# Sixteen of 22 blocks of each down projection as four jobs of seven products, with weight sums formed in DRAM

## The reference, cut to what matters

```python
def swiglu(hn, w_gate, w_up, w_down):
    return (jax.nn.silu(hn @ w_gate) * (hn @ w_up)) @ w_down   # w_down: 2816 x 1024
```

## Time and profile before

| | us |
|---|---|
| median of 3 runs | 2952.11 (2951.89 to 2953.47) |
| the profiled execution | 2952.24 |
| its span, first to last instruction | 2950.4 |
| TensorE busy in it | 2920.0 (99%) |
| VectorE, ScalarE, GpSimd busy | 1885.0, 1424.0, 1150.5 |
| DMA | 289.05 MB, mean 98 GB/s |

### The profile page before, as it was taken

The page is one execution under the profiler, slowest core; times in us unless marked ns, Lnnn a source line. Parts: engine busy times, 40 slices in busy tenths (PEclk is TensorE's granted clock), DMA queues, the critical chain, the costliest instruction groups (busy, mean ns, idle before and its releaser), DMA issues.

```text
span 2950.4 us, 44030 instructions
## 1 busy us (share of the span) xinstructions
PE 2920.0 (99%) x16942; PEld 2469.7 (84%) x16942; DVE 1885.0 (64%) x2718; ACT 1424.0 (48%) x2327; POOL 1150.5 (39%) x798
## 2 busy tenths in 40 slices
PE   8999999999999999999999999999999999999998
PEld 7778887799997877788888898988787888889987
DVE  7974333497885978772116888668777520288883
ACT  6443344455534546664234556344566532355553
POOL 5336575410124533234455214254332354541242
PEclk9999999999999999999999999999999999999999
DMA  5344343233323523223323234254231233333322
GB/s 163 86 115 138 94 129 103 75 115 104 97 81 87 148 72 102 55 72 89 97 90 105 78 113 127 79 123 135 70 94 48 71 97 98 97 97 100 101 94 79
DMA packets 221965, 289.05 MB, mean 98 GB/s; under 512 B 43466, under 2 KB 135682, under 8 KB 219970
## 3 DMA queue, kind: packets, MB, share of 16 engines
q1 hardware_dynamic: 219266, 281.07, 32.5%
q0 software_dynamic: 880, 2.99, 0.3%
q10 hardware_dynamic: 1616, 2.23, 0.2%
HBM read 270.98 MB, written 4.72 MB: 93 GB/s over the span
## 4 chain that ended last, share of the span: by engine, by line
PE 92%; DVE 5%; ACT 2%; issue 1%; POOL 0%; DMA 0%; SPq 0%; ACTq 0%; DVEq 0%
PE half L1063 66%; PE half L1392 4%; PE half L1394 4%; PE half L1395 4%; PE half L1581 2%; PE half L1595 2%; PE half L1559 1%; PE half L1466 1%; PE half L1468 1%; PE half L1469 1%; PE half L1564 1%; PE half L1657 0%; DVE arena L2752 0%; PE half L1318 0%; PE half L1335 0%
## 5 line engine op out<-in xcount | busy, mean ns | idle before, releaser
L4014 POOL TENSOR_TENSOR wL<-slot,wH 128x512 fp32r<-128x512 f32 x776 | 1125.0, 1459 | 1771.2 <-ACT wH L1781 1769.8
L1781 ACT ACTIVATE wH<-slot 128x512 fp32r<-128x512 f32 x776 | 475.4, 622 | 814.0 <-PE half L1063 786.4
L1063 PE MATMUL half<-nH,wH 128*128 128x512 f32 x1728 | 684.7, 396 | 4.2 <-ACT arena L1794 2.3
L1063 PE MATMUL half<-nH,wL 128*128 128x512 f32 x1728 | 673.5, 390 | 0.0
L1063 PE MATMUL half<-nL,wH 128*128 128x512 f32 x1728 | 673.3, 390 | 0.0
L1063 PE MATMUL half<-arena_split,wH 128*128 128x512 f32 (+1 forms) x2048 | 617.6, 384 | 0.8 <-POOL wL L4014 0.3
L1063 PEld LDWEIGHTS half<-arena_split,wH 128*128 128x128 f32 x2048 | 378.9, 188 | 78.6 <-POOL wL L4014 2.6
L1063 PEld LDWEIGHTS half<-nH,wH 128*128 128x128 f32 x1728 | 324.4, 188 | 87.1 <-issue 18.5
L1063 PE MATMUL half<-arena_split,wL 128*128 128x512 f32 (+1 forms) x1024 | 391.7, 383 | 0.0
L1063 PEld LDWEIGHTS half<-nH,wL 128*128 128x128 f32 x1728 | 324.4, 188 | 69.2
L1063 PEld LDWEIGHTS half<-nL,wH 128*128 128x128 f32 x1728 | 324.7, 188 | 65.4 <-issue 1.4
(11 more groups left out here) (480 smaller groups left out, 5287.7 us busy)
## 6 DMA issues: line engine op xcount, KB each, us to landing
slot<-in_w_in SPq DMA_DIRECT2D x344, 256.0 KB, 2.7
slot<-in_w_up SPq DMA_DIRECT2D x240, 128.0 KB, 2.2
arena<-in_w_up SPq DMA_DIRECT2D x200, 128.0 KB, 2.4
slot<-in_w_down SPq DMA_DIRECT2D x84, 256.0 KB, 3.9
slot<-in_w_branch SPq DMA_DIRECT2D x64, 256.0 KB, 2.6
slot<-in_w_out SPq DMA_DIRECT2D x48, 256.0 KB, 2.8
arena<-arena SPq DMA_DIRECT2D x40, 256.0 KB, 4.4
slot<-in_w_gate SPq DMA_DIRECT2D x48, 128.0 KB, 2.3
```

The costliest lines, as they stand in the source:

```text
L1063: mm = pe.matmul(dst, lhsT, rhs, start=(k == 0 and m == 0), stop=(k == last and m == 2))
L1781: act.activation(wH[:, p, 0:cols], slot[:, s, 0:cols], ACT.Copy).then_inc(weights_high, 1)
L4014: pool.tensor_tensor(wL[:, p, 0:cols], slot[:, s, 0:cols], plainly(wH[:, p, 0:cols]), ALU.subtract)\
```

## The change

`DENSE` falls from 14 to 6: blocks 0 to 5 stay dense, blocks 6 to 13 (group 0) and 14 to 21 (group 1) go into products. There are four jobs: `ds0` (group 0, columns 512 to 1023), `ds1` (group 0, columns 0 to 511), `ds2` (group 1, columns 0 to 511), `ds3` (group 1, columns 512 to 1023). `dn0` and `dn1` have six units each.

The weight sums S1 to S4 are no longer made by VectorE. For each down projection SyncE copies eight pieces of 512 by 512 within DRAM (`down_copy`), woven into earlier weight loads, and GpSimd issues eight adding DMAs in three steps (`down_accumulate`), each step behind a semaphore wait on the one before. They are placed in the first block after the units of `wk`, `wv` and `wq`, in a layer after those of `wo0`, `up0` and `up1`.

Each of the 28 weight operands is now loaded whole by one DMA of 512 KB into one of ten places (`down_load`), the first six once `up10` has been used, the others as places come free. VectorE's and ScalarE's lists in the down projection are new; so are the loads of `dn1` and the order at the end of the last layer.

```diff
-DOWN = [("dn0", 14, 1), (None, 2, 0)] + [(f"ds{j}", 7, 0) for j in range(2)] + [("dn1", 14, 1)]
+DOWN = [(None, 4, 0), ("dn0", 6, 1), (None, 2, 0)] + [(f"ds{j}", 7, 0) for j in range(4)] + [("dn1", 6, 1)]
-DENSE = 14
-DOWN_HALF = (1, 0)
+DENSE = 6
+DOWN_GROUP, DOWN_HALF = (0, 0, 1, 1), (1, 0, 0, 1)
+DOWN_WHOLE = 10
 ...
+            def down_copy(run, n):
+                g, of = divmod(n, len(DOWN_SUM))
+                half, out_half = ((0, 1), (0, 0), (0, 0), (1, 0))[of]
+                rows = src[ds(r0 + P * DENSE + D * g + T * half, T), :].rearrange("r (h i c) -> r h i c", h=2, i=2)
+                sp.dma_start(sums_kept[run, g, of].rearrange("r (h c) -> r h c", h=2), rows[:, :, out_half, :]).then_inc(S["sums_copied"], 16)
 ...
+            def down_load(stage, src, r0, l=0):
+                sp.wait_ge(S["sums_added"], 16 * 8 * (run_of(stage, l) + 1))
+                for u in range(DENSE):
+                    sp.wait_ge(landed[ring.slot[(f"{stage}dn0", u)]], ring.at(ring.landed, f"{stage}dn0", u, l, 0))
+                done(sp, f"{stage}up{NG - 1}", l)
+                for n in range(4 * len(PRODUCTS)):
+                    ...
+                    sp.dma_start(to, rows.rearrange("(k p) c -> p k c", p=P)).then_inc(sem, 16)
 ...
             for k in range(DENSE - 3):
                 unit(o, "bdn1", k, split(ff_high, ff_rests), 1)
-                if k == DENSE - 8:
+                if k == DENSE - 4:
                     fill("bout0", 1)
 ...
             def down_highs(stage, l=0):
+                done(act, f"{stage}up{NG - 1}", l)
+                round_units(dense, l, 0, [4], 512)
+                tokens_high(stage, 0, "B21", l)
+                tokens_high(stage, 0, "T3", l)
+                round_units(dense, l, 0, [5], 512)
+                down_high(stage, 0, l)
+                down_high(stage, 1, l)
+                tokens_high(stage, 0, "B22", l)
+                tokens_high(stage, 0, "T4", l)
+                after = {9: ["B11"], 13: ["T1", "T2"], 14: ["T4", "T3"], 15: ["B21"], 16: ["B22"]}
+                for n in range(2, 28):
+                    down_high(stage, n, l)
+                    ...
+                    for what in after.get(n, []):
+                        ...
+                        tokens_high(stage, 1, what, l)
 ...
-            round_units("bdn1", 1, 0, range(SPLITS, 11), 512)
             act.wait_ge(S["out_turned"], 1)
             evac(o_out[:, :, 0:T], banks(jobs.half["bout0"]), jobs.half["bout0"])
-            round_units("bdn1", 1, 0, range(11, DENSE), 512)
+            round_units("bdn1", 1, 0, range(SPLITS, DENSE), 512)
 ...
             def down_jobs(stage, l=0):
+                token_work = {0: [(0, "B22")], 1: [(0, "T4")], 11: ["T1", "T2", (1, "B11")], 12: ["T4", "T3"], 13: [(1, "T1")],
+                              14: [(1, "T2")], 15: [(1, "B21")], 16: [(1, "T3")], 17: [(1, "B22")], 18: [(1, "T4")]}
+                for n in range(28):
+                    j, nth = divmod(n, 7)
+                    if n + 2 < 28 and nth == 0:
+                        down_rest(stage, n + 2, l)
+                    if n == 0:
+                        down_dense(stage, l)
+                    elif nth == 0:
+                        down_add(stage, j - 1, 6, l)
+                        down_drained(stage, j - 1, l)
+                        ...
+                    else:
+                        down_add(stage, j, nth - 1, l)
+                        if n + 2 < 28:
+                            down_rest(stage, n + 2, l)
+                    for of in token_work.get(n, []):
+                        ...  (a name: down_token_sum of group 1; a pair: down_token_rest)
 ...
+            def down_accumulate(run, step):
+                pool.wait_ge(S["sums_copied"], 16 * 8 * (run + 1))
+                if step:
+                    pool.wait_ge(S["sums_added"], 16 * (8 * run + 2 + 2 * step))
+                ...
+                        pool.dma_start(of[n].rearrange("r (h c) -> r h c", h=2), rows, accum_op=ALU.add, max_dma_last_dim=1024)
```

More of the change, by code:

```diff
@@ L240 @@
               "xs0=0", "xs1=0", "xt0=0", "xt1=0", "xv0=0", "xv1=0", "xs2=0", "xs3=0", "xt2=0", "xt3=0", "xv2=0", "xv3=0",
-              "xo0=1", "xo1=0", "up0=1", "ss_ff=0"] + [f"up{g}={1 - g % 2}" for g in range(1, NG)] + ["dn0=0", "ds0=1", "ds1=0", "dn1=1"]
+              "xo0=1", "xo1=0", "up0=1", "ss_ff=0"] + [f"up{g}={1 - g % 2}" for g in range(1, NG)] + ["dn0=0", "ds0=1", "ds1=0", "ds2=1", "ds3=0", "dn1=1"]
 JOBS_LAYER = ["mix1=0", "ss_at=1", "qB=1", "mix2=0", "ix1=0", "ix2=0", "ix3=0", "lf=0", "qA=1", "kA=0", "vA=1",
@@ L245 @@
              [f"{s}{n}b" for n in range(4) for s in ("gt", "br")] + ["wo0=1", "wo1=0", "up0=1", "ss_ff=0"] + [f"up{g}={1 - g % 2}" for g in range(1, NG)]
-JOBS_DOWN = [["dn0=0", "ds0=1", "ds1=0", "dn1=1"], ["dn0=0", "ds0=1", "ds1=0", "out0=0", "dn1=1", "ss_fin=0"]]
+JOBS_DOWN = [["dn0=0", "ds0=1", "ds1=0", "ds2=1", "ds3=0", "dn1=1"], ["dn0=0", "ds0=1", "ds1=0", "ds2=1", "ds3=0", "out0=0", "dn1=1", "ss_fin=0"]]
 PAIRS = 4
@@ L918, in _ @@
             layer_vecs(0)
-            load("adn0", lin(I["w_down"], 0, 0), units=range(SLOTS))
-            done(sp, f"aup{NG - 1}")
-            down_quad("ads0", I["w_down"], 0)
-            load("adn0", lin(I["w_down"], 0, 0), units=range(SLOTS, DENSE))
-            all_split(sp, "adn0")
-            down_quad("ads1", I["w_down"], 0)
+            load("adn0", lin(I["w_down"], 0, 0))
+            down_load("a", I["w_down"], 0)
             down_last("a", I["w_down"], 0)
@@ L3449, in down_rest @@
-            def down_rest(stage, j, what, l=0):
-                dve.wait_ge(weights_high, ring.at(ring.before, f"{stage}ds{j}", PRODUCTS.index(what), l, 0) + 1)
-                high, low = down_weights(j, what)
-                rest(low, down_whole(j, what), high).then_inc(S["down_split"], 1)
+                out = down_tokens_whole(g, what)
+                if other:
+                    ins = dve.scalar_tensor_tensor(out=out, in0=down_tokens_whole(g, other), scalar=-1.0,
+                                                   in1=down_blocks(ff_raw, g, {"T2": "B22", "T4": "B21"}[what]), op0=ALU.mult, op1=ALU.subtract)
+                else:
+                    a, b = {"T1": ("B11", "B12"), "T3": ("B22", "B12")}[what]
+                    ins = dve.tensor_tensor(out, down_blocks(ff_raw, g, a), down_blocks(ff_raw, g, b), ALU.subtract)
@@ new lines, in down_token_sum, with down_token_rest, down_rest @@
+                ins.then_inc(S["down_tokens_summed"], 1)
+            def down_token_rest(stage, g, what, l=0):
+                dve.wait_ge(S["down_tokens_high"], 7 * down_group(stage, g, l) + DOWN_HIGHS[g].index(what) + 1)
+                high, low = down_tokens(g, what)
+                rest(low, down_tokens_whole(g, what), high).then_inc(S["down_tokens_split"], 1)
+            def down_rest(stage, n, l=0):
+                j, nth = divmod(n, 7)
+                dve.wait_ge(weights_high, ring.at(ring.before, f"{stage}ds{j}", nth, l, 0) + 1)
+                high, low = down_weights(j, PRODUCTS[nth])
+                rest(low, down_whole(j, PRODUCTS[nth]), high).then_inc(S["down_split"], 1)
@@ L3529, in _ @@
+                down_add(stage, 3, 6, l)
+                down_drained(stage, 3, l)
             whole_rest(2)
-            whole_rest(3)
+            down_token_sum("a", 0, "T1")
+            down_token_sum("a", 0, "T2")
             gated(f"aup{NG - 1}")
-            for g in range(4, DENSE // 2):
-                whole_rest(g)
             down_begun("a")
+            down_token_rest("a", 0, "B11")
+            down_token_rest("a", 0, "T1")
+            down_first("a")
             down_jobs("a")
@@ L3976, in _ @@
                 down_begun("b", l)
+                down_first("b", l)
                 down_jobs("b", l)
```

305 lines of the change are left out of this document (141 added, 164 removed).

## The result

The change makes the kernel slower: 3014.95 us (median of 4 runs, 3014.83 to 3016.11) against 2952.23 us for the kernel before on the same chip, a ratio of 1.0213 [1.0195, 1.023], 62.7 us. The sign was right, and the size was not: 2963.4 was forecast, with 2982 as the end of the range. In the profiled run the span is 3013.0 us, and the mean granted clock of TensorE 0.989, where the kernel before had 0.999.

The account below looks back on a forecast made before the run. The prediction took TensorE, busy 99%, to bound the kernel. It summed 2952.2 - 9.6 (queue) + 15.6 (middle) + 0.4 + 0.8 (starts) + 4.0 (end) = 2963.4 us, range 2948 to 2982.

Parts of the forecast that it names:

- What the change takes off: TensorE's queue in the down projections: 3.2 us less per projection, 9.6 us in all.
- P6's gap: TensorE's wait in ds0 for an add by VectorE, 1.08 us against the even pace; forecast to stay unchanged.
- The adds at 0, 0 to 5 us a layer: GpSimd's adding DMAs: taken at 0, with ends of 0 and some 5 us per layer.
- GpSimd is held by the adds: Rival, chance 0.10: slow adds hold the wait before up1's and up2's rests; 2975 to 3060 us.
- The cover: Dense work hiding the adds' moving: in a layer 16 units, 43.5 us, before GpSimd's next wait.
- Issues blocked by VectorE: Rival, chance 0.05: each add's issue waits for a VectorE instruction, 2.5 us lost three times; 2970.9 us.
- The middle: Group 1's token work from step 11: TensorE waits at products 13, 15, 16; 5.2 us per projection, 15.6 in all.
- the rival that the middle would run through: Chance 0.15: ScalarE and VectorE are further ahead there, only the end and starts cost; 2947.8 us.
- The lower bound of 1.2 us: Middle's cost per projection if only the overload beyond one add's slack counts.
- The end: Last layer's dn1: unit 5 is rounded behind the emptying of PSUM, so TensorE gets it late; +4.0 us.
- The start of ds0 and dn0: Late rests in the first block, +0.4 us; dn0's unit 5 rounded behind T3 in layers, +0.4 us each.
- The loads and copies at 0: Weight loads by DMA and SyncE's copies within DRAM: both forecast to cost nothing.

Follow-up runs that it names:

- e10: e8 with all eight copies of a layer issued by the fourth branch load, and dn0's last unit rounded ahead of T3's high part; 2944.97 us, 0.997.
- e1: Kernel after without its 24 adding DMAs and the written waits between their steps, sums left unfinished; 2973.92 us, 1.0072 of the kernel before.
- e2: Kernel after without the 24 adding DMAs and the 24 copies, loading blocks of w_down where sums would be loaded; 2973.85 us.
- e6: Kernel after with all 24 adds issued singly, each behind earlier ones and at least five dense units later, none at wk and wv; 2977.76 us, 1.008.
- e5_start_end: Kernel after with ScalarE rounding dn0's first four units ahead of T2's high part in layers, and last dn1's last two units earlier; 3010.85 us.
- e8: Kernel after with e5_start_end's and e6's edits, the middle's token work spread evenly, and VectorE adding P1 before dn0; 2951.72 us, 0.9993.
- e9: Kernel after with the program argument dynamic_dma_scratch_size set to 8192; 3044.28 us, one run.

## Why the prediction was wrong, point by point

**What the change takes off: right.** With the gaps gone, e10 is 8.9 us below the kernel before. The count of 9.6 for TensorE's queue and the 3 x 1.08 of P6's gap (which the change did not touch) make 12.8. Of the 3.9 us between, 1.4 stand in one new gap at the start of the first layer's attention, where VectorE waits longer for four DMAs that exchange partitions (`arena<-arena`, median landing 5.0 us in place of 4.1). It is in e1 and e2 too, so neither adds nor copies cause it. About 1 us is at the very start of the profiled run. The rest I can't assign.

**The adds at 0, 0 to 5 us a layer: this is the step that failed.** They measured 41.0 us. The rival "GpSimd is held by the adds" had the right engine, but a chance of 0.10 and a condition that never came about: it wanted four adds to take over 49.6 us, and they landed within 36.7. That the time lies inside its span of 2975 to 3060 is luck. Three things in the step were wrong.
- *The cover.* It was taken as "16 units (43.5 us) before the next wait" for a layer, and that was right there: the written wait cost nothing in either layer. For the first block it was never worked out. There the 16 units are those of wv, 21.8 us, with GpSimd busy 21.5 of them. The four issues alone opened 3.98 us at 436, and the wait 12.35 us at 473.
- *The issue.* One add takes 1.27 us alone and four in a row 5.30, where 0.93 and 3.7 were taken from line 4033: still within 6.1 us in a layer.
- *The hold.* That GpSimd can stand at an issue until an earlier add has landed was not in the sum or among the rivals. The kernel before has no adding DMA at all, so it could not be read there; two plain loads that GpSimd issued at 5.8 and 6.8 us, each landing in over 7 us, were under way together without a hold. It cost 8.85 us at 1658 and 3.78 at 2655; the third hold falls in the first block's attention, where GpSimd has time.

The rival "Issues blocked by VectorE" (2970.9) did not come about: four issues in a row took 5.30 us for its 8.6. The longest issue of an add was 2.93 us, at the end of four in a row, and single ones took 1.25 to 1.31 us in e6, nine of them with VectorE busy beside them throughout.

**Gaps priced at their length: a term that was missing.** Behind each gap of 3.1 us and more of the kernel after, but for the one of 5.41 us at 8.61 us of the span (clock 1.00 behind it), the granted clock was half for 3.0 to 5.9 us, which took 1.5 to 2.8 us more each. That happens eight times: at 436, 473, 1658 and 2655 behind GpSimd, in the three middles and at the end. It makes some 6.4 us of the middle's 20.1.

**The middle: right in place and size.** Forecast 0.9, 3.6 and 0.7; measured 0.94, 3.29 and nothing at product 16, in all three projections, charged to the rest named in the forecast. It came to 4.55 us per projection against the even pace, and 6.7 with the clock, for 5.2. The reading was of the lists, by the row of each instruction. Against the rival that the middle would run through spoke only the written order, and that was enough. The lower bound of 1.2 us was a slip, since its own terms (26.7 - 23.0 - 2.2) make 1.5; nothing hung on it.

**The end: right.** 3.13 us charged to `wL` (3.3 against the even pace) for a forecast of 4.0, and 1.7 for the clock on top.

**The start of ds0 and dn0: half right.** Each 0.4 us of the forecast stands behind a working that makes 0.3. In the first block P6's gap grew from 0.92 to 1.55 us, 0.6 for the 0.4 forecast. In the layers dn0's last unit was forecast 0.4 late because it is rounded behind T3. It was not late, since something ahead of it was later: ScalarE waits for VectorE's T2 before it rounds dn0's first four units, 1.60 us. In the kernel before they were rounded well ahead, and I had not followed that move. With it mended the forecast's place appeared at once, with 1.48 us in e5_start_end. ScalarE there:

```profile
1847.87 1.06 ACT L2274 ACTIVATE arena_split<-arena 128x1024 fp32r<-128x1024 f32 x1 [0.20 <-DVE arena L3449]
1848.83 2.17 ACT L1810 ACTIVATE wH<-slot 128x512 fp32r<-128x512 f32 x4
```

**The loads and copies at 0: right**, but for the loads of w_up that land beside an adding DMA: 2.5 us in the second layer.

**The sum mended.** With the rest taken from the starts of the matmuls, 2963.4 + 41.0 (adds by the medians, with the slower stretches behind their gaps) + 4.5 (middle, 20.1 for 15.6) + 2.7 (dn0's start, 3.5 for 0.8) + 0.2 (P6 in the first block) + 1.0 (end, 5.0 for 4.0) + 1.4 (attention) = 3014.2, for 3014.95. That is as close as medians from several chips allow.

## What to carry to other kernels

- Price an asynchronous operation by who queues behind its issue, in the narrowest place where it is issued. A cover of so many units is worth only what those units leave the issuing engine free. The same four adds and the wait behind them cost nothing at the first layer's wo, and opened gaps of 16 us behind wk and wv.
- If a trace doesn't show two of an operation under way at once, how they hold each other is an unknown with a price of its own, here about one landing time each (holds of 9.1 to 11.3 us, landings of 10.1 to 12.4 us). Issue them apart until a trace says otherwise.
- A gap on TensorE can cost more than its length: eight of the nine of 3.1 us and more in the kernel after took 1.5 to 2.8 us besides, in a slower stretch behind them. And a first unit that waits hides how late the next one is, so mend both before reading the gain.

## What the runs showed of the hardware

- A DMA that adds 1 MB in DRAM landed in 9.0 to 14.1 us alone (e6, e8, e10). Four in a row landed one after another, each 10.0, 20.5, 30.4 and 36.7 us behind its own issue (kernel after, at 430).
- Without `dynamic_dma_scratch_size` in the program GpSimd was held three times in 24 adds, 30.4 us in all (kernel after), and with 8192 six times, 68.1 us (e9, one run). It was never held with the adds one at a time (e6, e10).
- A load issued by SyncE beside an add under way landed in a median of 6.8 us in place of 2.5 (128 KB, e8_all). The 24 copies of 1 MB, issued by SyncE, left the time as it was (2973.92 us with them in e1, 2973.85 without in e2).
- After TensorE had stood for 3.1 to 12.4 us it was granted half its clock for 3.0 to 5.9 us, eight times of nine in the kernel after; the ninth is the gap of 5.41 us at 8.61 us of the span, with a clock of 1.00 behind it. In e5 it was not, after 3.48 us, and was after 1.85 us. After the gaps of 1.6 us and less in the kernel after its matmuls started at the even pace at once.
